# Prompt softmax with the mask added by TensorE, exponentials read from PSUM, and the division folded into the transposing product

## The reference

```python
def block(args):                      # 128 queries of the prompt
    sc = indexer_scores(qib, wb, ki)
    sc = jnp.where(pos[None, None, :] <= pb[None, :, None], sc, -jnp.inf)
    _, sel = lax.top_k(sc, topk)      # 64 keys per query
    valid = sel <= pb[None, :, None]
    return sparse_attend(qb, gather_rows(k, sel), gather_rows(v, sel), valid)

def sparse_attend(q, ks, vs, valid):
    s = jnp.einsum('btngd,btknd->btngk', qg, ks) * HEAD_DIM ** -0.5
    s = jnp.where(valid[:, :, None, None, :], s, -jnp.inf)
    p = jax.nn.softmax(s, axis=-1)
    return jnp.einsum('btngk,btknd->btngd', p, vs)
```

## Time and profile before

| | |
|---|---|
| median of three runs | 1151.5 us (1150.71 to 1151.86) |
| the profiled execution | 1149.91 us, span 1148.3 us |
| TensorE busy | 1082.8 us, 94% |
| VectorE busy | 741.7 us, 65% |
| ScalarE busy | 514.2 us, 45% |
| GpSimd busy | 190.1 us, 17% |
| mean granted TensorE clock | 0.982 |

### The profile page before, as it was taken

One profiled execution on the slowest core, in us unless ns is written; L12 is line 12 of the kernel. 1 busy time (PEld: TensorE's weight loads), 2 busy tenths in 40 slices (PEclk: granted clock), 3 DMA queues, 4 the chain that ended last, 5 costly groups with the idle time before them and its releaser, 6 DMA issues.

```text
span 1148.3 us, 27626 instructions
## 1 busy us (share of the span) xinstructions
PE 1082.8 (94%) x9358; PEld 1025.1 (89%) x9358; DVE 741.7 (65%) x1211; ACT 514.2 (45%) x832; POOL 190.1 (17%) x241
## 2 busy tenths in 40 slices
PE   6999999999779999999999999999986799999996
PEld 6999999888448999999999999998863699999996
DVE  5676744788955766764476776448888466676544
ACT  5544433621444644443464444345215455444432
POOL 4211100411300311110041111004222022111001
PEclk9999999999879999999999999999998899999998
DMA  8464565343536355555435465563444445555541
GB/s 279 163 231 165 199 234 189 138 139 131 151 94 178 129 183 183 181 185 178 154 110 206 172 217 202 193 224 124 123 137 138 93 139 184 182 180 177 189 149 38
DMA packets 90465, 191.17 MB, mean 166 GB/s; under 512 B 12323, under 2 KB 48483, under 8 KB 90403
## 3 DMA queue, kind: packets, MB, share of 16 engines
q1 hardware_dynamic: 87426, 184.82, 48.7%
q0 software_dynamic: 2976, 5.53, 2.0%
HBM read 187.71 MB, written 2.59 MB: 166 GB/s over the span
## 4 chain that ended last, share of the span: by engine, by line
PE 85%; DVE 5%; ACT 3%; SPq 2%; issue 2%; DMA 1%; POOL 0%; DVEq 0%; POOLq 0%; ACTq 0%
PE PS L1105 23%; PE PS L1106 23%; PE PS L1107 23%; PE PS L1213 4%; SPq L263 2%; PE PS L1243 2%; PE PS L1141 2%; DVE w_lo L599 1%; PE PS L1153 1%; PE PS L1152 1%; PE PS L1156 1%; DVE rstd_post L628 1%; ACT w_hi L379 1%; PE PS L1454 1%; PE PS L1357 1%
## 5 line engine op out<-in xcount | busy, mean ns | idle before, releaser
L599 DVE TENSOR_TENSOR w_lo<-raw,w_hi 128x1024 fp32r<-128x1024 f32 x295 | 394.7, 1339 | 312.3 <-ACT w_hi L379 309.8
L379 ACT ACTIVATE w_hi<-raw 128x1024 fp32r<-128x1024 f32 x295 | 310.7, 1055 | 240.5 <-PE PS L1107 212.1
L1105 PE MATMUL PS<-x_hi,w_hi 128*128 128x264 f32 x1456 | 415.7, 286 | 0.7 <-DVE w_lo L599 0.6
L1106 PE MATMUL PS<-x_lo,w_hi 128*128 128x264 f32 x1456 | 412.5, 283 | 0.0
L1107 PE MATMUL PS<-x_hi,w_lo 128*128 128x264 f32 x1456 | 412.4, 283 | 0.0
L1105 PEld LDWEIGHTS PS<-x_hi,w_hi 128*128 128x128 f32 x1456 | 274.2, 188 | 2.3 <-DVE w_lo L599 1.6
L1106 PEld LDWEIGHTS PS<-x_lo,w_hi 128*128 128x128 f32 x1456 | 274.4, 188 | 0.1
L1107 PEld LDWEIGHTS PS<-x_hi,w_lo 128*128 128x128 f32 x1456 | 273.0, 187 | 0.0
L1105 PE MATMUL PS<-h_hi,w_hi 128*128 (+1 forms) x832 | 237.1, 285 | 3.4 <-issue 3.3
L1107 PE MATMUL PS<-h_hi,w_lo 128*128 (+1 forms) x832 | 236.9, 285 | 0.0
L1106 PE MATMUL PS<-h_lo,w_hi 128*128 (+1 forms) x832 | 236.2, 284 | 0.0
(11 more groups left out here) (255 smaller groups left out, 1000.2 us busy)
## 6 DMA issues: line engine op xcount, KB each, us to landing
raw<-in_wts SPq DMA_DIRECT2D x312, 512.0 KB, 3.6
kv<-in_kT SPq DMA_DIRECT2D x128, 64.0 KB, 2.0
kx<-in_kxT SPq DMA_DIRECT2D x128, 32.0 KB, 2.1
vx<-in_vC POOLq DMA_DIRECT2D x48, 64.0 KB, 2.5
raw<-in_vC SPq DMA_DIRECT2D x32, 64.0 KB, 2.3
kv<-in_vC SPq DMA_DIRECT2D x32, 64.0 KB, 1.9
out_yT<-h SPq DMA_DIRECT2D x8, 132.0 KB, 1.8
vx<-in_vC SPq DMA_DIRECT2D x16, 64.0 KB, 1.9
```

The lines of the kernel that those rows point to most:

```text
L379: act.activation(w_hi[:, u % SPLIT, :], raw[:, u % RAW, :], ACT.Copy) \
L599: tt(w_lo[:, u % SPLIT, :], raw[:, u % RAW, :], w_hi[:, u % SPLIT, :].bitcast(F32), AL.subtract) \
L1105: pe.matmul(out, w_hi[:, w, cols], hi, start=start, stop=False)
L1106: pe.matmul(out, w_hi[:, w, cols], lo, start=False, stop=False)
```

## The change

`scores(j)` now puts three products into each piece of a bank: the scores, then `hide` (-1e30 on the diagonal) times `bias`, then the identity times the causal mask from the constants. `bias` holds only the indexer's choice. The masked scores stay in PSUM; VectorE takes the maxima there, and ScalarE reads its exponentials from there and writes `sp_`. Head pairs alternate between banks 2, 3 and banks 6, 7 (`SCORES`). `norm(j)` no longer scales `sp_`; it writes `share`, four matrices of 128 x 128 that hold the reciprocals on their diagonal, and the transposes become true products of `sp_` with `share`. They all go to bank 0, the second half when the first has been copied. `fold` and the channel sums move to bank 1, and the first product with the values waits for the square root (`c_rms`) that reads it.

```diff
-        nc01 = place("nc01", [128, 384], F32)
+        hide = place("hide", [128, 128], F32)
+        share = place("share", [128, 4, 128], F32)
...
+        SCORES = (2, 6)
...
                 def exps(j):
                     act.wait_ge(sem["s_masked"], at_layer(L, "s_masked", j + 1))
+                    if j >= 2:
+                        act.wait_ge(sem["p_t"], at_layer(L, "p_t", 2 * j - 2))
                     for a in range(2):
                         for b, (lo, hi) in enumerate(((0, 256), (256, 384))):
-                            t = sp_[:, j % 2, a, lo:hi]
-                            ins = act.activation(t, t, ACT.Exp, scale=SCALE,
+                            ins = act.activation(sp_[:, j % 2, a, lo:hi], PS[:, SCORES[j % 2] + a, lo:hi], ACT.Exp,
+                                                 scale=SCALE,
...
-                        act.activation(pT[:, a, :], PS[:, (7, 0)[a], 0:384], ACT.Copy).then_inc(sem["p_tc"], 1)
+                        act.activation(pT[:, a, :], PS[:, 0, 0:384], ACT.Copy).then_inc(sem["p_tc"], 1)
...
-                stt(bias1[:, :], wk1[:, :], TAKEN / 2, nc01[:, 0:256], AL.is_gt, AL.add)
-                after(L, step(L, stt(bias0[:, :], wk0[:, :], TAKEN / 2, nc01[:, 256:384], AL.is_gt, AL.add)))
+                ts(bias1[:, :], wk1[:, :], TAKEN / 2, None, AL.is_gt)
+                ts(bias0[:, :], wk0[:, :], TAKEN / 2, None, AL.is_gt).then_inc(sem["mask_p"], 1)
 
                 def masked(j):
                     dve.wait_ge(sem["s_p"], at_layer(L, "s_p", j + 1))
-                    if j >= 2:
-
-                        dve.wait_ge(sem["p_t"], at_layer(L, "p_t", 2 * j - 2))
-                    s = sp_[:, j % 2, :, :]
-                    linked(stt(s, bias[:, :].unsqueeze(1).to_broadcast([128, 2, 384]), -BIG, PS[:, 2:4, 0:384],
-                               AL.mult, AL.add))
+                    s = PS[:, SCORES[j % 2]:SCORES[j % 2] + 2, :]
...
-                    for b, (lo, hi) in enumerate(((0, 256), (256, 384))):
-                        t = sp_[:, j % 2, :, lo:hi]
-                        ins = tt(t, t, sps[:, j % 2, b:4:2].unsqueeze(2).to_broadcast([128, 2, hi - lo]), AL.mult)
-                    ins.then_inc(sem["p_norm"], 1)
+                    if j:
+
+                        dve.wait_ge(sem["p_t"], at_layer(L, "p_t", 2 * j))
+                    tt(share[:, :, :], ident.unsqueeze(1).to_broadcast([128, 4, 128]),
+                       sps[:, j % 2, :].unsqueeze(2).to_broadcast([128, 4, 128]), AL.mult).then_inc(sem["p_norm"], 1)
...
-            ts(nc01[:, 0:256], con[:, C_CA1:C_CA1 + 256], -1 / BIG, None, AL.mult)
-            ts(nc01[:, 256:384], con[:, C_CA0:C_CA0 + 128], -1 / BIG, None, AL.mult)
+            ts(hide[:, :], ident, -BIG, None, AL.mult)
...
                         pe.wait_ge(sem["rope"], at_layer(L, "rope", 8))
+                        pe.wait_ge(sem["mask_p"], at_layer(L, "mask_p", 1))
                         pe.wait_ge(sem["c_part"], at_layer(L, "c_part", 1))
+                    elif j == 1:
+                        pe.wait_ge(sem["s_masked"], at_layer(L, "s_masked", 1))
+                        pe.wait_ge(sem["c_part"], at_layer(L, "c_part", 4))
+                        pe.wait_ge(sem["v_nat"], at_layer(L, "v_nat", 1))
                     else:
-                        pe.wait_ge(sem["s_masked"], at_layer(L, "s_masked", j))
+                        pe.wait_ge(sem["p_exp"], at_layer(L, "p_exp", j - 1))
                     for a in range(2):
                         rows = slice(64 * a, 64 * a + 64)
-                        pe.matmul(PS[:, 2 + a, 0:256], aq[rows, j, 128:256], ak[rows, 0:256], start=True, stop=True)
-                        ins = pe.matmul(PS[:, 2 + a, 256:384], aq[rows, j, 0:128], ak[rows, 0:128],
-                                        start=True, stop=True)
+                        for lo, n, q0, seen in ((0, 256, 128, C_CA1), (256, 128, 0, C_CA0)):
+                            out = PS[:, SCORES[j % 2] + a, lo:lo + n]
+                            pe.matmul(out, aq[rows, j, q0:q0 + 128], ak[rows, 0:n], start=True, stop=False)
+                            pe.matmul(out, hide[:, :], bias[:, lo:lo + n], start=False, stop=False)
+                            ins = pe.matmul(out, ident, con[:, seen:seen + n], start=False, stop=True)
                     ins.then_inc(sem["s_p"], 1)
...
                     for a in range(2):
-                        if j:
-                            pe.wait_ge(sem["p_tc"], at_layer(L, "p_tc", 2 * j - 1 + a))
-                        elif a == 0:
-
-                            pe.wait_ge(sem["conv_p"], at_layer(L, "conv_p", 1))
+                        if j or a:
+                            pe.wait_ge(sem["p_tc"], at_layer(L, "p_tc", 2 * j + a))
                         else:
 
                             pe.wait_ge(sem["chunk"], at_layer(L, "chunk", 15))
-                        p = sp_[:, j % 2, a, :]
-
                         for n, c in enumerate((256, 0, 128)):
-                            ins = pe.transpose(PS[:, (7, 0)[a], 128 * n:128 * n + 128], p[:, c:c + 128], ident)
+                            ins = pe.matmul(PS[:, 0, 128 * n:128 * n + 128], sp_[:, j % 2, a, c:c + 128],
+                                            share[:, 2 * a + c // 256, :], start=True, stop=True)
                         ins.then_inc(sem["p_t"], 1)
...
                     if j:
                         pe.wait_ge(sem["o_lo"], at_layer(L, "o_lo", j))
+                    else:
+                        pe.wait_ge(sem["c_rms"], at_layer(L, "c_rms", 1))
```

More of the change, by code:

```diff
@@ L499, in mixer @@
                 for c in range(2):
-                    ins = act.activation(cacc[:, c, 0:NP], PS[:, 7, NP * c:NP * c + NP], ACT.Identity,
+                    ins = act.activation(cacc[:, c, 0:NP], PS[:, 1, NP * c:NP * c + NP], ACT.Identity,
                                          bias=pars[:, DWB + c:DWB + c + 1])
@@ L526, in mixer @@
                             act.wait_ge(sem["o_p"], at_layer(L, "o_p", j))
-                        act.activation(pT[:, a, :], PS[:, (7, 0)[a], 0:384], ACT.Copy).then_inc(sem["p_tc"], 1)
+                        act.activation(pT[:, a, :], PS[:, 0, 0:384], ACT.Copy).then_inc(sem["p_tc"], 1)
                     if j == 0:
                         act.wait_ge(sem["c_var"], at_layer(L, "c_var", 1))
-                        act.activation(crs[:, :], PS[:, 6, 0:NT], ACT.Sqrt, scale=1.0 / 256,
+                        act.activation(crs[:, :], PS[:, 1, 0:NT], ACT.Sqrt, scale=1.0 / 256,
                                        bias=epsb[:, 0:1]).then_inc(sem["c_rms"], 1)
@@ L960, in centred @@
                     for c in range(2):
-                        ins = stt(cacc[:, c, :], PS[:, 6, 0:NT], -1.0 / 256, cacc[:, c, :], AL.mult, AL.add)
+                        ins = stt(cacc[:, c, :], PS[:, 1, 0:NT], -1.0 / 256, cacc[:, c, :], AL.mult, AL.add)
                     ins.then_inc(sem["c_cent"], 1)
@@ L1253, in fold @@
                     for i in range(4):
-                        ins = pe.matmul(PS[32 * i:32 * i + 32, 7, :], stack[:, :], cpart[:, i, :],
+                        ins = pe.matmul(PS[32 * i:32 * i + 32, 1, :], stack[:, :], cpart[:, i, :],
                                         start=True, stop=True)
@@ L1378, in channel_sum @@
                     for c in range(2):
-                        ins = pe.matmul(PS[:, 6, 0:NT], ones, t[:, c, :], start=(c == 0), stop=(c == 1))
+                        ins = pe.matmul(PS[:, 1, 0:NT], ones, t[:, c, :], start=(c == 0), stop=(c == 1))
                     ins.then_inc(sem[name], 1)
```

1 line of the change is left out of this document (removed).

## The result

The changed kernel takes 1203.88 us (median of 4 runs, 1201.98 to 1209.77), the kernel before 1151.11 on the same chip: ratio 1.0464 [1.0426, 1.0503], 52.8 us slower. The prediction was 1179 (1165 to 1190). The profiled execution, with a span of 1208.1 us, is the slowest of the four (1209.77); sums inside the trace are made against that span and 1148.3 of before.

The account below looks back on a forecast made before the run. The prediction took TensorE as the bound, with SyncE's key transfers leading the attention middle. Two layers' 27 us plus 1 for the clock gave 28 on 1149.9, 1177.9, so about 1179 beside the median (range 1165 to 1190).

Parts of the forecast that it names:

- The wait of `keys(1)` for its transfer: Attention middle: key transfers end at 321.2, TensorE reaches `keys(1)` later still, so this wait disappears.
- four `scores` are in series: Each layer's attention middle: all four `scores` end up in series on TensorE, 3.5 us more each, 14 per layer.
- the sum: Layer path from TensorE's start to the sample softmax: +14.0 us in layer 0, +13.0 in layer 1, at full clock.
- the second halves wait: Transposing products sharing bank 0: second half waits for ScalarE's copy, some 3 and 2 us for j = 1, 2.
- Only the key transfers matter: Rival: scores overlap other engines' work, transfers ending at 321.2 set `keys(1)`; 9 us in all, 1160; chance 0.10.
- Faster: Rival: mask products cost well under half, `scores` under about 1.5 us, fuller clock gains at most 2.5 per layer, 1146.5; chance 0.04.
- Nothing: Rival: VectorE's gains and TensorE's losses are both hidden, so the change does nothing; chance 0.03.
- the third: Rival: every tile-shape change drains, or half clock sits on the scores; +17 to 20 per layer, 1186 to 1192; chance 0.13.
- The size of `scores`: Score and mask products on TensorE: 4.4 us per `scores`, the middle of 3.9 and 4.8, against 0.93 before.
- What was said of the drain: Tile-shape changes in `scores`: the skill's drain rule would give 5.3 us or so, the trace row 4.4; prediction followed the row.
- The half clock: TensorE after 2 to 3.5 us idles: one half-rate stretch over a `scores` costs up to 1.7 us; 0.5 added per layer.

Follow-up runs that it names:

- filled: Changed kernel plus unneeded products in TensorE's three waits inside the transposing pairs, for j = 0, 1 and 2: 1187.49 us, 1.0329 of the kernel before.
- no_shape_change: Changed kernel with the four score products also on all 128 rows, so output differs: 1180.47 us, 1.0290 of the kernel before.
- division_only: Kernel before with only the division moved into the transposing product, its two banks kept: 1148.60 us, ratio 0.9982.
- mask_only: Kernel before with only the mask moved to TensorE, in old banks 2 and 3, exponentials reading PSUM: 1197.59 us, ratio 1.0414.
- scores_paired: Changed kernel, same 12 products, both head halves of a piece before their masks, 4 row changes instead of 8: 1182.01 us, 1.0278 of the kernel before.
- scores_first: Changed kernel with all four score products before all masks, 2 row changes, sums not the reference's: 1175.19 us, 1.0211 of the kernel before.
- combined: Changed kernel with one mask product in float32r, paired order and ScalarE's copies ahead of the next exponentials: 1163.14 us, 1.0110 of the kernel before.

## Why the prediction was wrong

**Right: the mechanism and the path.** The wait of `keys(1)` for its transfer is gone; fold and `keys(0)` stand behind `scores(0)`; four `scores` are in series, with nothing of VectorE's between them but the maxima that the sum has; the second halves wait 3.0 and 1.8 us for ScalarE's copy (forecast 3 and 2); what lies outside the two gaps did not change beyond 1.5 us (59.8 − 58.3). Of the rivals, *Only the key transfers matter*, *Faster* and *Nothing* are out: `scores` is over 4.4 us, not under it, and `keys(1)` starts at 344.56 (forecast 331 to 333) without a wait for its transfer. Nearest is the third, which named both causes, drains and half clock, but as alternatives; both came. Its 1186 to 1192 is what the kernel takes with the drains alone (filled: 1187.5). So two terms of the sum failed, in their size.

**The size of `scores`, the first step that failed: 4.4 was 5.46.** Streaming was right (3.9; no_shape_change has 4.10 with its two ends). The step from one kind of product to the next was put between 0 and 0.1 us (the bounds 3.9 and 4.8), and is 0.20. The error is in the reading of the earlier trace rows. The prediction took 299.86 to 300.72 for two steps, found 0.2 us lost and halved it. The same rows of before, with what stands on either side:
```profile
299.32 0.61 PE L1357 MATMUL PS<-kv,LA 128*32 128x512 f32 x4
299.86 0.71 PE L1371 MATMUL PS<-ak,aq 64*128 64x256 f32 x4
300.40 0.39 PE L1372 MATMUL PS<-ak,aq 64*128 64x128 f32 x4
300.72 1.16 PE L1379 MATMUL PS<-cacc,con 128*128 128x264 f32 x4
```
The last 128x32 products start at 299.32 and the next thing 0.54 later, where such groups are otherwise 0.43 apart (298.03 to 299.32 is three such steps): 0.11 lost ahead of 299.86. From there to 300.72 it is 0.86 for 0.65 of streaming: 0.21 lost. Behind 300.72 four records end after 1.16, where three steps of 0.222 and the last record's 0.39 make 1.06: 0.10 lost. So each of the two changes (from 128x32 to 64 rows, and from 64 rows to 128) costs about 0.2, half of it ahead of the first record on the new rows and half behind it, and the window that was read holds one half of each. The change in after costs the same, so the rows of before had its price.

By the prediction's own chain, which has each of the four `scores` once, 5.46 + 5.39 + 5.49 + 5.49 = 21.8 us stand in place of 17.6: 4.2 per layer, 8.5 in all. The trace of filled bears this out: its gaps are 46.0 us in both layers, and the sum has 41.9 (337.6 − 295.77, and 0.1 to the softmax), so 4.1 each are missing and `scores` explains them.

**What was said of the drain.** The prediction held that the trace disagrees with the Trainium skill ("TensorEngine Tiling (Array Packing)", section "Key Properties": a change of tiling mode drains TensorE), because a 64-row product starts at 299.86 and the records before it run to 299.93. But records of neighbours overlap where nothing changes, too: in no_shape_change one product starts at 295.06 and lasts 0.59, and the next starts at 295.50, 0.15 before its end. At 299.86 the overlap is 0.07. The row shows a delay, not its absence, and the runs agree with the page in that each change costs time: the 5.3 us that the prediction gave for the rule is nearer to the 5.46 measured than its 4.4.

**The half clock, the second step that failed and the larger one.** "One half-rate stretch over a `scores` costs up to 1.7 us. I add 0.5 per layer." It cost 15.9 us by the medians, and some 23 in the profiled execution (58.3 less the 35.1 by which filled's gaps stand over before's: 18.1 and 17.0). No row gives the 1.7: the earlier trace rows has a stretch of 3.7 us at the low level, and a `scores` of 4.4 us that lies wholly in one would take 4.4 more by the prediction's own numbers. The prediction took the low level for something that follows an idle wait and is over after a few microseconds. Four of eight `scores` were at or partly at 0.50, a whole one 4.5 us longer (10.0 against 5.46), and in layer 1 the level held through `scores(2)`, `scores(3)` and most of `keys(1)`. The idle waits were forecast, with their place and length; what stands behind them, at twice its duration, was not multiplied out.

Together: the sum had 27 us at full clock and 1 for the clock. Measured are 36.9 and 15.9, 52.8 in all. Of the 24.8 too much, 8.5 is `scores`, 14.9 is the clock, and 1.4 was not traced to a term and is within the noise of the medians.

**The division by itself**, on which the prediction spent little, is worth next to nothing: division_only takes 1148.6 us (-0.18%), so VectorE's saving and the longer transposing products do not show as long as the keys' transfers lead.

## What to carry to other kernels

Moving an elementwise pass onto the matmul engine is a trade of an idle engine's time for the bound engine's; price the added products with the order they stand in, since each change between 64 and 128 rows here costs as much as a 256-column record, and group products of one shape. Where a plan leaves the matmul engine idle for 2 to 3 us, price what stands behind the wait at both clock levels, and try filling the wait with products into unused columns: the medians fell by 16.4 us here, of which a part may be a difference between executions, and by 7.4 in the kernel before. And when a row seems to contradict a rule, compare the starts on both sides of the step with the same products where there is no step; the ends of records overlap anyway, and a window cut at the step itself holds only a half of what the step costs.

## What the runs showed of the hardware that was not expected

- TensorE was busy for 10.00 of 10.00 us at a granted clock of 0.50, and in mask_only for 25.20 of 27.30. The Trainium skill's page "TensorE: Matmul & The Clock Gate", section "Part 1: The HAM clock gate (the "warmup" mystery)", has the clock up when the array is busy; the rows of this mix of shapes do not bear that out, those of filled do.
- A change between 64-row and 128-row products costs 0.20 us at full clock (scores_paired 4.07 against scores_first 3.67, two changes apart), about half of it ahead of the first record on the new rows and half behind it.
- Products that nobody needs, run by TensorE in its waits, make a kernel faster: 1149.02 to 1141.66 us.
- The operands' data made no difference to the clock that the time shows (1202.99 against 1203.88 us).
- A `float32r` mask product is recorded once where float32 is recorded twice, and takes half as long: in combined two products of 256 columns are 2 records in 0.43 us, a single float32 one in no_shape_change takes 0.43.
- Exponentials of a head pair take 1.72 us from PSUM and 1.87 from SBUF.
